# A two-layer trunk with routed experts: the residual inside the first expert, counting behind the selection, norms per token tile, norm rows on two strips

## The reference, cut to what matters

```python
for l in range(2):
    sh1, sc1, g1, sh2, sc2, g2 = split(silu(c) @ w_ada[l] + b_ada[l])
    h = x * (1 + sc1) + sh1
    y = conformer_conv(h, ...) if l == 0 else fox_attention(q, k, v, fcum) @ w_o
    x = layer_norm(ALPHA * x + (1 + g1) * y, ln_mix_g[l], ln_mix_b[l])
    h = x * (1 + sc2) + sh2
    y = grouped_moe(h, router_w, router_b, w_gate[l], w_up[l], w_down[l])
    x = layer_norm(ALPHA * x + (1 + g2) * y, ln_ffn_g[l], ln_ffn_b[l])
```

## Time and profile before

| what | us |
|---|---|
| median of 3 runs | 1350.45 |
| lowest and highest of them | 1350.08, 1356.78 |
| the profiled execution, its own time | 1354.81 |
| its span, first to last instruction | 1353.1 |
| mean granted PE clock | 0.923 |
| PE busy in the span | 1102.8 |
| DVE, ACT, POOL busy | 430.4, 169.1, 21.1 |
| bytes moved | 494.74 MB, mean 366 GB/s |

### The profile page before, as it was taken

One profiled execution on the slowest core, in us unless ns is written; L12 is line 12 of the kernel. 1 busy time (PEld: TensorE's weight loads), 2 busy tenths in 40 slices (PEclk: granted clock), 3 DMA queues, 4 the chain that ended last, 5 costly groups with the idle time before them and its releaser, 6 DMA issues.

```text
span 1353.1 us, 30933 instructions
## 1 busy us (share of the span) xinstructions
PE 1102.8 (82%) x13118; PEld 653.6 (48%) x13118; DVE 430.4 (32%) x1378; ACT 169.1 (12%) x411; POOL 21.1 (2%) x61
## 2 busy tenths in 40 slices
PE   4999989669997689666999979695699996796666
PEld 2885345335554245333575853562356663453333
DVE  0697252113332123111472332431133231231114
ACT  1113130001010001000201420300010110000001
POOL 1300000000000000000000000000000000000000
PEclk9899979889999899888999989598899998998888
DMA  9985599999999999999995433789999899999990
GB/s 356 385 319 226 226 426 422 425 423 425 426 426 423 426 424 424 425 425 422 414 414 231 173 125 134 302 361 422 424 427 426 337 411 424 425 425 424 424 413 37
DMA packets 56959, 494.74 MB, mean 366 GB/s; under 512 B 4196, under 2 KB 12420, under 8 KB 17176
## 3 DMA queue, kind: packets, MB, share of 16 engines
q1 hardware_dynamic: 55920, 490.75, 87.5%
q10 hardware_dynamic: 744, 2.35, 0.5%
q0 software_dynamic: 192, 0.15, 0.0%
HBM read 492.19 MB, written 1.05 MB: 365 GB/s over the span
## 4 chain that ended last, share of the span: by engine, by line
PE 56%; DMA 36%; DVE 4%; ACT 2%; issue 2%; SPq 0%; DVEq 0%; POOLq 0%
PE PS L1079 24%; DMA ring<-in_w_up_dram 21%; DMA ring<-in_w_gate_dram 8%; PE PS L977 6%; PE PS L1201 4%; DMA ring<-in_w_down_dram 3%; PE PS L1107 3%; PE PS L884 3%; DMA work<-in_w_gate_dram 2%; PE PS L1058 2%; PE PS L994 2%; PE PS L1325 2%; DMA ring<-in_w_ada_dram 2%; PE PS L1070 1%; PE PS L1372 1%
## 5 line engine op out<-in xcount | busy, mean ns | idle before, releaser
L1079 PE MATMUL PS<-ring,work 128*32 128x256 f32 x8160 | 519.7, 411 | 171.7 <-DMA ring<-in_w_up_dram 71.6
L1079 PEld LDWEIGHTS PS<-ring,work 128*32 128x32 f32 x8160 | 282.7, 117 | 393.9 <-issue 121.2
L1641 DVE TENSOR_TENSOR work<-work,PS 128x256 f32<-128x256 f32 x47 | 19.8, 422 | 452.9 <-PE PS L1079 452.9
L977 PE MATMUL PS<-ring,work 128*128 128x512 f32 x192 | 83.4, 594 | 0.5 <-ACT work L818 0.5
L686 ACT ACTIVATE work<-PS 128x256 f32<-128x256 f32 x47 | 18.0, 383 | 449.8 <-PE PS L1079 449.8
L1079 PE MATMUL PS<-work 128*32 128x256 f32 x864 | 54.5, 394 | 16.9 <-DMA work<-in_w_gate_dram 8.5
L884 PE MATMUL PS<-ring,cact 128*32 128x512 f32 x384 | 50.3, 662 | 16.5 <-DMA ring<-in_w_ada_dram 16.5
L1201 PE MATMUL PS<-work,ring 128*128 128x256 f32 x256 | 58.1, 390 | 2.2 <-ACT work L623 2.2
L1058 PE MATMUL PS<-hs,work 128*32 128x256 f32 x784 | 56.2, 406 | 3.8 <-DVE work L1609 3.8
L1107 PE MATMUL PS<-work 32*128 32x256 f32 x784 | 56.2, 400 | 3.8 <-DVE work L1654 3.8
L977 PEld LDWEIGHTS PS<-ring,work 128*128 128x128 f32 x192 | 36.3, 190 | 46.4 <-issue 45.6
(11 more groups left out here) (254 smaller groups left out, 881.9 us busy)
## 6 DMA issues: line engine op xcount, KB each, us to landing
ring<-in_w_gate_dram SPq DMA_DIRECT2D x58, 2048.0 KB, 34.1
ring<-in_w_up_dram SPq DMA_DIRECT2D x58, 2048.0 KB, 34.9
ring<-in_w_down_dram SPq DMA_DIRECT2D x58, 2048.0 KB, 28.0
ring<-in_w_ada_dram SPq DMA_DIRECT2D x24, 2048.0 KB, 20.8
work<-in_w_up_dram SPq DMA_DIRECT2D x6, 2048.0 KB, 19.4
work<-in_w_gate_dram SPq DMA_DIRECT2D x6, 2048.0 KB, 34.1
work<-in_w_down_dram SPq DMA_DIRECT2D x6, 2048.0 KB, 42.5
ring<-in_w_pw_dram SPq DMA_DIRECT2D x8, 1024.0 KB, 12.1
```

Of the source, the lines that this page charges most:

```text
L977: last = pe.matmul(PS[:, banks + 2 * t + q, :], moving[:, k, t * P:(t + 1) * P], quarter(index + h, kk, KH)[:, q * BANK:(q + 1) * BANK], s ...
L1079: last = pe.matmul(dst[SLOTS * s:SLOTS * (s + 1), :], rows[:, cc, SLOTS * q:SLOTS * (q + 1)], quarter(load + h, kk, KH)[:, QUART * s:QUART ...
```

## The change

Seven edits, in the order of the program:

1. The norm rows are loaded to two strips: first halves at rows 72 to 79, second halves at 104 to 111. That makes eight loads of them in place of four on ACT's queue, and the matrix product that makes columns of them (L1190) takes its 16 columns from the two places.
2. `turn_h` goes tile by tile: the eight transposes of tile 0, then the eight of tile 1; each bank is signalled in the second pass. `turn_n` waits per tile behind the first norm of a layer; behind the second norm it waits for both tiles, as before. The norm's pieces are made and signalled per tile.
3. ACT and DVE signal their copies on semaphores of their own, and `w_pw1` and the first query wait for pairs of columns as they come to them. The router and K wait for everything, as before.
4. ACT computes columns 0 and 1 of `rT` ahead of its copy of the logits (`rT_begun`), the other six where all eight were, and then touches Silu with one column (`warm`).
5. In layer 0, two pieces of `w_ada_kv` stand ahead of the counting matmuls and two behind them, in place of three and one; their result is in bank 0 and waits for `rT_begun`.
6. The residual stands, in both layers, in expert 0 between the hidden products of all its blocks and its results. In layer 1 it no longer stands ahead of the counting matmuls, in layer 0 no longer ahead of the first gather.
7. The wait for `ada_added` 4 moves from ahead of expert 0 to just ahead of the residual.

```diff
-                load_rows(NORM_ROW + 4 * n, w.rearrange("l (h n) -> (l h) n", n=BANK))
+                for h in range(2):
+                    load_rows(NORM_ROWS[h] + 2 * n, w[:, h * BANK:(h + 1) * BANK])
...
-                            last = act.activation(hs_chunks(t, 1), sums_chunks(t, 1), ACT.Identity, bias=negm[:, t:t + 1],
-                                                  scale=rstd[:, t:t + 1])
-                        last.then_inc(n_half, 1)
+                            act.activation(hs_chunks(t, 1), sums_chunks(t, 1), ACT.Identity, bias=negm[:, t:t + 1],
+                                           scale=rstd[:, t:t + 1]).then_inc(n_half, 1)
                         return
-                    act.activation(chunks(hs, 1)[:, 1], by_chunk(xs[:, 1, :])[:, 1], ACT.Identity, bias=negm[:, 1:2],
-                                   scale=rstd[:, 1:2]).then_inc(n_half, 1)
+                    for t in range(TT):
+                        act.activation(chunks(hs, t)[:, 1], by_chunk(xs[:, t, :])[:, 1], ACT.Identity, bias=negm[:, t:t + 1],
+                                       scale=rstd[:, t:t + 1]).then_inc(n_half, 1)
...
+                residual_T(range(2), rT_begun)
                 act.wait_ge(logits_parted, 2 * l + 1)
                 act.activation(parts[:, 0, :], PS[:, B_GATE, 0:SEQ], ACT.Copy).then_inc(parts_kept, 1)
                 act.wait_ge(lmax_ready, l + 1)
                 act.activation(r_ex[:, :, :], r_ex[:, :, :], ACT.Exp).then_inc(lexp_ready, 1)
+                residual_T(range(2, KD), rT_ready)
+                act.activation(warm[:, :], cact[:, 0:1], ACT.Silu)
...
-                spread_row(lambda i: NORM_ROW + 4 * n + 2 * l + i, bank)
+                spread_row(lambda i: NORM_ROWS[i] + 2 * n + l, bank)
...
+            def turn_h(chunk, norms=None):
+                for t in range(TT):
+                    if norms is not None:
+                        of_sums = norms % 2 == 0
+                        pe.wait_ge(h_ready, TT * (norms - 1) + (TT if of_sums else t + 1))
+                        pe.wait_ge(n_half, TT * (norms - 1) + (TT if of_sums else t + 1))
+                    for k in range(KD):
+                        last = pe.transpose(PS[:, k // 2, (k % 2) * SEQ + t * P:(k % 2) * SEQ + (t + 1) * P],
+                                            chunk(t, k), ident[:, :])
+                        if t == TT - 1 and k % 2 == 1:
+                            last.then_inc(h_turned, 1)
...
-                    for j in range(ADA_G - 1):
-                        ada_load(L_ADAKV, j, B_GATE)
-                else:
-                    residual()
+                    pe.wait_ge(rT_begun, 1)
+                    for j in range(2):
+                        ada_load(L_ADAKV, j, 0)
 
                 pe.wait_ge(sel_ready, l + 1)
...
                 if l == 0:
-                    ada_load(L_ADAKV, ADA_G - 1, B_GATE)
-                    residual()
+                    for j in range(2, ADA_G):
+                        ada_load(L_ADAKV, j, 0)
...
-                if l == 0:
-                    pe.wait_ge(ada_added, 4)
                 for e in range(E):
...
                     with pe.Fori(0, blocks):
                         hidden_of(pe.snap(n_pe) + 1, index + 6 * e)
                         pe.reg_add(n_pe, n_pe, 1)
+                    if e == 0:
+                        if l == 0:
+                            pe.wait_ge(ada_added, 4)
+                        residual()
                     with pe.Fori(0, blocks):
...
+                        if f == g == 0 and k % 2 == 0:
+                            h_there(k)
...
+                    if i == 0 and k % 2 == 0:
+                        h_there(k)
+                        if k == 0:
+                            h_there(2)
...
-                    dve.tensor_scalar(chunks(hs, 1)[:, 0], by_chunk(xs[:, 1, :])[:, 0], mv[:, 1, 0:1], rstd[:, 1:2],
-                                      ALU.subtract, ALU.mult)
-                    dve.tensor_scalar(chunks(hs, 0), by_chunk(xs[:, 0, :]), mv[:, 0, 0:1], rstd[:, 0:1],
-                                      ALU.subtract, ALU.mult).then_inc(h_ready, 1)
+                    for t in range(TT):
+                        dve.tensor_scalar(chunks(hs, t)[:, 0], by_chunk(xs[:, t, :])[:, 0], mv[:, t, 0:1], rstd[:, t:t + 1],
+                                          ALU.subtract, ALU.mult).then_inc(h_ready, 1)
```

More of the change, by code:

```diff
@@ L624, in copy_hT @@
                                               bias=shift[:, k:k + 1], scale=scale[:, k:k + 1])
-                    last.then_inc(hT_copied, 1)
+                    last.then_inc(hT_by_act, 1)
                 turned[0] += 1
@@ L670, in moe, with residual_T @@
             def moe(l):
+                def residual_T(chunks_of, done):
+                    for k in chunks_of:
+                        last = act.activation(rT[:, k, :], PS[:, k // 2, (k % 2) * SEQ:(k % 2 + 1) * SEQ], ACT.Identity,
+                                              bias=rescol[:, 2 + l, k:k + 1], scale=rescol[:, l, k:k + 1])
+                    last.then_inc(done, 1)
+                residual_T(range(2), rT_begun)
                 act.wait_ge(logits_parted, 2 * l + 1)
@@ L674, in moe @@
                 act.activation(r_ex[:, :, :], r_ex[:, :, :], ACT.Exp).then_inc(lexp_ready, 1)
-                for k in range(KD):
-                    last = act.activation(rT[:, k, :], PS[:, k // 2, (k % 2) * SEQ:(k % 2 + 1) * SEQ], ACT.Identity,
-                                          bias=rescol[:, 2 + l, k:k + 1], scale=rescol[:, l, k:k + 1])
-                last.then_inc(rT_ready, 1)
+                residual_T(range(2, KD), rT_ready)
+                act.activation(warm[:, :], cact[:, 0:1], ACT.Silu)
                 def take_x(n):
```

53 lines of the change are left out of this document (24 added, 29 removed).

## The result

The changed kernel takes 1340.53 us (median of 6 runs, 1337.55 to 1343.95) against 1352.88 for the kernel before (6 runs, 1349.97 to 1356.78). The ratio is 0.991, 95% interval 0.9887 to 0.9934: 12.3 us or 0.9% faster; in microseconds the interval runs from 8.9 to 15.3 and leaves out no change. The forecast was 1342.0 within 1338.5 to 1347.5, so the time fell inside. The gain was forecast at 8.5, just under that interval. That the time came within 1.5 of the forecast is partly luck: the forecast started from the median of three runs, 1350.45, and with six it is 1352.88, from which the same 8.5 would have given 1344.4. The profiled execution of after took 1339.30 (span 1337.5, mean granted clock 0.927), that of before 1354.81 (1353.1, 0.923).

What follows compares the result with a forecast made beforehand. PE was taken to set the pace to 159.5 and from layer 0's experts to 883, transfers through layer 0's experts, both afterwards. 0.8 + 1.7 + 6.05 = 8.55, so 8.5 off 1350.45 gave 1342.0 us, range 1338.5 to 1347.5.

Steps and rivals of the forecast that it cites:

- Layer 1's counting: Layer 1's routing: without the residual ahead, counting follows the selection and the gather starts sooner; 6.05 us gained.
- The spreads: Norm-row spreads between the halves of K: two strips save 0.43 on each of four instruction pairs; 1.7 us gained.
- Tile by tile: Last turn in layer 1: banks are ready later, so DVE's two pairs run one behind the other; 0.35 us lost.
- The first product: `w_pw1` at the start: PE waits for two of ACT's copies, not four, starting 0.97 earlier; 0.8 us gained.
- The extra loads: Four more issues on ACT's queue at the start delay only things read long after; 0, or 4.1 us without that cover.
- Layer 0's routing: Layer 0: PE saves 4 to 5 us before expert 0, but full DMA transfers hide it; counted as 0.
- rival B: Layer 0 counts too: if PE held its transfers somewhere, 4.8 us more arrive, giving 1337.2 us; chance 0.07.
- The residual in its new place: Inside expert 0: costs 3.79 us at full clock or 7.09 at half, hidden under 8.7 us of cover; 0.
- The clock: Routing gap: the residual ran at half clock throughout, so removing it takes no speed from the experts; no term.
- Rival A: Layer 1's routing gain does not arrive, being used up before expert 0 or at the second hole; 1348.0 us, chance 0.17.

Runs made afterwards that it cites:

- the tripled spreads: Changed kernel with norm rows in one strip again and the two norm spreads between the halves of K made three times each: 1365.16 us, ratio 1.0068.
- the first kernel that has them: Changed kernel plus eight unread dense products in layer 1's routing gap, five ahead of the wait for the selection, three behind the counting: 1337.05 us, ratio 0.9879.
- the same products in the second: Changed kernel plus the eight unread dense products, with layer 1's last turn, ahead of the router, bank by bank again: 1340.93 us, ratio 0.9906.

## Why the prediction was right, and where its sum was not

**Layer 1's counting, 6.05: confirmed in the changed kernel.** With the residual put back it loses 5.5 in the trace and 5.6 to 6.0 in medians (8.5 by the ratios). On the kernel before, the same edits gave only 1.8 in the median. Before to after the same stretch shrank by 8.12 (22.24 to 14.12). The rest, 2.6, is 1.68 of clock at the router (1.93 + 1.86 less 1.07 + 1.04), a stretch that I had left at its old clock, and 0.92 that also stands in the kernel with the residual put back: it waits 3.72 for ACT's columns, not 4.64, since two of them are made ahead.

**The spreads, 1.7: mechanism right, size off.** The pair fell by 1.71, in every kernel with two strips. But the step "in one strip each instruction adds 0.43" priced only their own time. One strip can also pull the clock down: the second half of K took 15.70 and 16.96 in two of the four one-strip kernels with normal spreads, 14.01 in all nine profiles with two strips, and the tripled spreads show that one-strip spreads can do this. In the whole kernel the edit is worth 3.9 in medians (6.4 by the ratios).

**Tile by tile, 0.35 lost: right in the trace, open for the time.** The loss is there, 0.41 where all is at full clock (columns to router 5.71, against 5.30 in the kernels with edit 1 or edits 4 to 7 alone). Undoing the edits in the changed kernel nevertheless costs 3.5 in the median, of which its trace shows 1.67 between router and gather; adding them to the kernel before costs 3.8. Again the step priced the work itself, at one clock. That the tile-wise turn helps the clock is not shown: the router's first product ran at half clock in two of five profiles with the turn by banks and in one of nine with the turn by tiles, but the product behind it, the logits' sum, took 1.86 for 1.04 in two of the five and in five of the nine.

**The first product, 0.8: right in the copies, nothing in this profile.** PE starts 1.17 behind the copies for 1.98, so 0.8 was gained. The profile of after ran the last piece of the first weights at half clock, though, and gave it away; before and after, from the timelines:

```profile
29.58 1.92 PE L884 MATMUL PS<-ring,cact 128*32 128x512 f32 x16 [1.12 <-DMA ring<-in_w_ada_dram]
```

```profile
29.72 3.53 PE L893 MATMUL PS<-ring,cact 128*32 128x512 f32 x16 [2.55 <-DMA ring<-in_w_ada_dram]
```

In the second profile of the changed kernel this ran at full clock and `w_pw1` began at 35.87, the forecast's 35.8. But its first 64 products then took 16.96 for 16.17, and the first expert load went out at 159.41 for 159.54: only 0.13 of the 0.8 reached the transfers there. In the seven profiles with edits 1 to 3, the same program up to there, it lies between 157.63 and 161.09, so a gain of 0.8 at this place is not shown. The extra loads' price of 0 stands: nothing in front of the copies is later in that trace.

**Layer 0's routing, 0: right.** Expert 0 began 3.4 sooner (195.83 for 199.27), measured from the first expert load 5.0; the last up load of the layer was issued 1.7 later, as the first was. It moved with the first load, not with its expert. That refutes rival B as it was put. K does start 1.65 sooner behind that last load, by the clock of the last up half; this piece was slow in all three profiles without edits 4 to 7 and in two of eleven with them, so a part of the gain may come from layer 0 after all. Whether the edits or chance do that is open.

**The residual in its new place, 0: right,** with 9.5 of cover. The drain at a change of tiling mode, which the Trainium skill (TensorEngine Tiling (Array Packing), Key Properties) names, costs little to be seen here: in layer 1 the two transposes ahead of the residual start at 876.12, the residual at 876.49, and the next piece at 880.21, before the residual's 3.79 are out; the whole insertion takes 3.72 from start to start.

**The clock, 0: this was the mis-sized term.** I looked only at whether the removed residual had held the clock up (rightly not: 7.09 in every kernel with it there), and took everything else at the clock of before. By the sum, 8.5 were forecast and 12.3 came. The losses when one part is taken out, 5.6 for the counting, 3.9 for the spreads and 3.5 for the turns, make 13.0 in medians; by the ratios they are 8.5, 6.4 and 3.1, which make 18, so that 13.0 comes near 12.3 is no proof that the parts add up. Of the two last, 7.4 in all (9.5 by the ratios), I had 1.35. The traces show the clock's share at single places: 1.68 at the router, 1.69 in the second half of K, 3.2 at the two last up halves. How much of the 3.8 between forecast and medians each of them makes is not shown. The Trainium skill (TensorE: Matmul & The Clock Gate, Part 1) says that activity releases the throttle; the dense products of the first kernel that has them agree (their 4.54 + 2.82 us of work save 3.7). The residual's 7.09 us of busy PE that released nothing do not, nor does the clock of 0.58 behind the same products in the second.

**Rival A** did not come: the distance from the first down load to the end of the span was 470.1 before, 467.8 after, 471.3 in the second profile of after and 469.8 with the residual put back. Each stretch did hand its shift to the next, and of the differences 1.5 is the last up half.

**What stays open.** The parts do not add up from the other side: on the kernel before, edit 1, edits 4 to 7 and edits 2 and 3 give -1.0, -1.8 and +3.8 in medians. Each alone leaves the other places where the clock can fall, and the kernel before itself ranges over 10 us; that this is the reason is argued and not shown, since one execution of each was profiled. What lets the clock fall in one execution of a kernel and not in another was not tried. The attention stretch, from the second columns to the output product, was 78.06 before, 75.1 and 80.3 in two kernels close to it, 76.5 to 76.7 in seven profiles of the changed kernel and its variants, and 77.8 to 79.1 in the other four; what does this is open too.

## What to carry to other kernels

Cost an edit on TensorE twice: by its own time, and by what it does to the clock of the dense work behind it; look in the timeline for the same group at two durations in two kernels. Between dense stretches, avoid matmuls that use one strip of the array alone. A few dense products that nobody reads, placed ahead of a wait in a gap that bounds the kernel, were worth 3.7 us in one trace here, and nothing over the changed kernel when the clock had fallen just ahead of them. And find the hole in the transfers first: the 13.3 us by which the restart behind it came sooner all reached the end, while the 3.4 to 5 us by which expert 0 of layer 0 came sooner under full transfers did not move the last load of that layer.

## What the runs showed of the hardware, not expected

- A busy TensorE is not enough to keep the clock. One-strip matmuls (32 rows of the array) back to back let it fall to 0.50; two strips at a time, equally long, left it at 1.00. Sixty-four small matmuls (64 rows, 64 columns) that ran for 7.09 us at 0.50 left it there in four kernels, while the same 64, started at full clock inside an expert, ran at full clock for 3.79, and three times as many for 10.94.
- The same program meets the clock differently from one execution to the next. In the two profiles of the changed kernel the last up half of expert 15 in layer 1 took 1.93 and 3.13, and the last piece of the first weights 3.53 and 1.92.
- The times of one kernel spread by up to 12 us: the kernel before over 9 to 12 us (18 to 35 runs), the changed kernel over 3.6 to 6.4 (5 and 6 runs), the one with single strips over 10 (11 runs). The kernel with the dense products, whose profile has the clock at 1.00 all through the routing, spreads over 10 as well (6 runs), so a narrower spread is not shown to come with a steadier clock.
- Two loads of ACT's function tables show as 1.28 us each (ACT's timeline, 849.03 and 854.19), and nobody waited for them: the logits' sum on PE and DVE's selection ran beside them.
